# First norm of a decoder step on one Trainium2 core: raw rows transposed on arrival, the norm applied after the transposes, the kept rows added as the residual

## The reference

```python
def rmsnorm(x, g):
    xf = x.astype(jnp.float32)
    y = xf * lax.rsqrt(jnp.mean(xf * xf, axis=-1, keepdims=True) + EPS)
    return (y * g.astype(jnp.float32)).astype(x.dtype)

mp = mixer(rmsnorm(hp, norm_mix), ...)      # u @ w_in -> q, k, v, g, p, ga, gb; retention, pooling; @ w_out
hp = hp + mp                                # the residual
hp = hp + moe(rmsnorm(hp, norm_ffn), ...)   # top 4 of 32 experts, clamped SwiGLU
y  = rmsnorm(hp, norm_final)
```

## Time and profile before

| what | value |
|---|---|
| median of 3 runs | 1323.03 us (1321.56 to 1323.11) |
| the profiled execution, its own time | 1323.81 us |
| its span, first to last instruction | 1321.8 us |
| TensorE busy (matmul) | 1251.9 us, 95% |
| VectorE, ScalarE, GpSimd busy | 250.9, 168.0, 46.0 us |
| moved by DMA | 451.25 MB, mean 341 GB/s |

### The profile page before, as it was taken

One profiled execution on the slowest core, in us unless ns is written; L12 is line 12 of the kernel. 1 busy time (PEld: TensorE's weight loads), 2 busy tenths in 40 slices (PEclk: granted clock), 3 DMA queues, 4 the chain that ended last, 5 costly groups with the idle time before them and its releaser, 6 DMA issues.

```text
span 1321.8 us, 15582 instructions
## 1 busy us (share of the span) xinstructions
PE 1251.9 (95%) x5956; PEld 649.0 (49%) x5956; DVE 250.9 (19%) x579; ACT 168.0 (13%) x326; POOL 46.0 (3%) x81
## 2 busy tenths in 40 slices
PE   4999999998999999999999999999999999999984
PEld 3878678886434344443434344443434343443432
DVE  0143311203021211112121211212021211112022
ACT  3122211003101101110100110110100101001102
POOL 3014310000000000000000000000000000000000
PEclk9999999997899999999999999999999999999987
DMA  9552775431699999999999999999999999999980
GB/s 294 191 192 96 242 253 207 159 114 66 253 363 421 414 422 414 420 416 418 419 415 421 414 421 415 421 415 419 417 417 419 414 422 414 422 415 420 416 330 34
DMA packets 108060, 451.25 MB, mean 341 GB/s; under 512 B 7321, under 2 KB 38085, under 8 KB 75128
## 3 DMA queue, kind: packets, MB, share of 16 engines
q1 hardware_dynamic: 104704, 439.56, 83.0%
q0 software_dynamic: 3328, 11.30, 2.6%
HBM read 444.99 MB, written 6.08 MB: 341 GB/s over the span
## 4 chain that ended last, share of the span: by engine, by line
PE 77%; DMA 18%; DVE 2%; ACT 1%; issue 1%; SPq 0%; DVEq 0%; ACTq 0%
PE psum L780 23%; DMA ring<-in_w_down 18%; PE psum L727 18%; PE psum L796 15%; PE psum L819 11%; PE psum L845 5%; PE psum L809 1%; PE psum L834 1%; DMA tok<-in_meta_tokens 1%; PE psum L683 1%; PE psum L731 0%; PE psum L651 0%; PE psum L781 0%; PE psum L668 0%; PE psum L915 0%
## 5 line engine op out<-in xcount | busy, mean ns | idle before, releaser
L780 PE MATMUL psum<-ring,x_T 128*64 128x512 f32 x1024 | 462.3, 599 | 0.7 <-ACT x_T L1014 0.7
L781 PE MATMUL psum<-ring,x_T 128*64 128x512 f32 x1024 | 462.3, 599 | 0.0
L780 PEld LDWEIGHTS psum<-ring,x_T 128*64 128x64 f32 x1024 | 134.1, 137 | 273.3 <-issue 272.2
L796 PE MATMUL psum<-ring,act_T 128*64 128x512 f32 x1024 | 236.1, 603 | 25.3 <-DMA ring<-in_w_down 22.0
L727 PE MATMUL psum<-u_T,ring 128*128 128x264 f32 (+1 forms) x704 | 169.3, 395 | 0.0
L819 PE MATMUL psum<-one_hot,normed 128*128 128x128 f32 (+1 forms) x816 | 152.2, 317 | 1.2 <-DVE one_hot L1273 1.2
L796 PEld LDWEIGHTS psum<-ring,act_T 128*64 128x64 f32 x1024 | 73.3, 138 | 151.5 <-issue 145.8
L727 PEld LDWEIGHTS psum<-u_T,ring 128*128 128x128 f32 x704 | 131.6, 191 | 28.9 <-issue 3.5
L819 PEld LDWEIGHTS psum<-one_hot,normed 128*128 128x128 f32 (+1 forms) x816 | 115.5, 195 | 56.2 <-issue 27.7
L781 PEld LDWEIGHTS psum<-ring,x_T 128*64 128x64 f32 x1024 | 134.2, 137 | 0.0
L1343 DVE TENSOR_TENSOR z_T<-z_T,psum 128x264 f32<-128x264 f32 x136 | 58.3, 429 | 207.2 <-PE psum L845 206.1
(11 more groups left out here) (215 smaller groups left out, 544.1 us busy)
## 6 DMA issues: line engine op xcount, KB each, us to landing
ring<-in_w_gate_up SPq DMA_DIRECT2D x256, 1024.0 KB, 19.5
ring<-in_w_down SPq DMA_DIRECT2D x128, 1024.0 KB, 19.4
ring<-in_w_in SPq DMA_DIRECT2D x22, 1024.0 KB, 5.2
ring<-in_state_ret POOLq DMA_DIRECT2D x8, 512.0 KB, 6.2
out<-ring POOLq DMA_DIRECT2D x8, 512.0 KB, 4.3
ring<-in_w_ret_branch SPq DMA_DIRECT2D x4, 1024.0 KB, 5.0
ring<-in_w_out SPq DMA_DIRECT2D x4, 1024.0 KB, 5.0
ring<-in_w_pool_branch SPq DMA_DIRECT2D x2, 1024.0 KB, 8.0
```

The costliest lines, as they stand in the source:

```text
L780: mm(psum[0:CAP, 2 * j + n], x, slot(s)[:, n * 512:(n + 1) * 512], start=k == 0, stop=k == KD - 1)
L781: last = mm(psum[CAP:P, 2 * j + n], x, slot(s)[:, D + n * 512:D + (n + 1) * 512], start=k == 0, stop=k == KD - 1)
L796: last = mm(psum[j * CAP:(j + 1) * CAP, 4 + n], act_T[:, j, 2 * q + f], w[:, f * D + n * 512:f * D + (n + 1) * 512], start=q == 0 and f == ...
```

## The change

- The raw rows are transposed, tile by tile as each lands, all eight blocks into eight PSUM banks. ScalarE copies each block unscaled into a new buffer `x_kept` (1024 x 280, transposed). `tok` now lies in the space of `vk`, and is not needed after the head.
- The squares run beside this, three tiles, then one root instruction for all. VectorE's reciprocals are turned by three matmuls (reciprocals broadcast, times the identity) into a row that stands on all partitions, copied to `rstd_row`. VectorE then writes `u_T` = `x_kept` x `norm_mix` x `rstd_row`.
- The identity and eps come first in `consts` and are loaded alone by ScalarE's queue, the rest by SyncE's behind the second weight chunk. The four parameter rows move from GpSimd's queue to ScalarE's. x is loaded as two DMAs with their own semaphores. SyncE no longer waits for the parameter rows. An early root on ScalarE's stream brings its table in.
- The expert-bias transposes become an auxiliary job behind tile 4.
- In tiles 64 to 71 the identity matmuls go. VectorE adds `x_kept` while it takes the tile out into `y_T`; ScalarE scales that into `xn_T`. The waits for the bank and the logits follow.

```diff
+_aux(4, ("b_gu",), (7,))
-for _n, _w in (("ident", 128), ("before", 128), ...
-               ("of_row", NS), ("eps", 1)):
+for _n, _w in (("ident", 128), ("eps", 4), ("before", 128), ...
+               ("of_row", NS)):
+EARLY = CONST["before"][0]
-        tok = msb("tok", 3 * D).rearrange("p (t d) -> p t d", t=3)
+        x_kept = msb("x_kept", KD * NA).rearrange("p (k t) -> p k t", k=KD)
+        tok = vk[:, 0:3 * D].rearrange("p (t d) -> p t d", t=3)
+        rstd_row = win_all[:, 0:NA]
 ...
-            elif n < T_OUT:
+            else:
                 eng.wait_ge(dve_took, n - T_YB + 1)
-            else:
-                eng.wait_ge(act_took, T_YB + n - T_OUT + 1)
 SyncE
-            sp.dma_start(tok[:, 0:2, :], x_prompt[0].rearrange("(t p) d -> p t d", p=P)).then_inc(x_in, 16)
-            sp.dma_start(consts[:, :], ins["consts"]).then_inc(consts_in, 16)
-            sp.wait_ge(cleared, 1)
-            sp.dma_start(tok[0:NS, 2, :], x_sample.rearrange("b s d -> (b s) d")).then_inc(x_in, 16)
-            sp.dma_start(tok[32:32 + NM, 2, :], meta).then_inc(x_in, 16)
+            for t in range(2):
+                sp.dma_start(tok[:, t, :], x_prompt[0, t * P:(t + 1) * P, :]).then_inc(x_in[t], 16)
+            sp.wait_ge(cleared, 2)
+            sp.dma_start(tok[0:NS, 2, :], x_sample.rearrange("b s d -> (b s) d")).then_inc(x_in[2], 16)
+            sp.dma_start(tok[NS:NS + NM, 2, :], meta).then_inc(x_in[2], 16)
-            sp.wait_ge(rows_in, 4 * 16)
             for i in range(C_PB):
                 mix_chunk(i)
+                if i == 1:
+                    sp.dma_start(consts[:, EARLY:], ins["consts"][:, EARLY:]).then_inc(consts_in, 16)
 GpSimd
-            nc.gpsimd.memset(tok[0:64, 2, :], 0.0).then_inc(cleared, 1)
+            nc.gpsimd.memset(small[:, 0:4], 1.0).then_inc(cleared, 1)
+            nc.gpsimd.memset(tok[:, 2, :], 0.0).then_inc(cleared, 1)
-            for o, name, n in ((0, "norm_mix", 8), (8, "ret_gn", 8), (16, "pool_scale", 4), (20, "norm_ffn", 8)):
-                pool.dma_start(rows[o:o + n, 0:P], ins[name].rearrange("l (a p) -> (l a) p", p=P)).then_inc(rows_in, 16)
 TensorE, aux
+                elif kind == "b_gu":
+                    pe.wait_ge(b_gu_in, 16)
+                    for c in range(4):
+                        last = pe.transpose(banks(bank)[:, c * P:(c + 1) * P], rows[:, (1 + c) * P:(2 + c) * P], ident)
 TensorE, head (the loop quoted above and the b_gate_up transposes go)
-            pe.wait_ge(consts_in, 16)
+            pe.wait_ge(ident_in, 16)
             pe.wait_ge(rows_in, 4 * 16)
+            pe.transpose(psum[:, 7, 384:412], rows[0:28, 0:P], ident[0:28, 0:28]).then_inc(params_turned, 1)
+            for t in range(3):
+                pe.wait_ge(x_in[t], 32 if t == 2 else 16)
+                for k in range(KD):
+                    if t == 0 and k == KD - 1:
+                        pe.wait_ge(params_ready, 1)
+                    last = pe.transpose(psum[:, k, t * P:(t + 1) * P], tok[:, t, k * P:(k + 1) * P], ident)
+                    if t == 2:
+                        last.then_inc(x_turned, 1)
+            pe.wait_ge(rstd_ready, 1)
+            pe.wait_ge(kept, 1)
+            for t, n in enumerate((P, P, NS + NM)):
+                last = mm(psum[:, 0, t * P:t * P + n], rstd[:, t:t + 1].broadcast_to([P, P]), ident[:, 0:n], start=True,
+                          stop=True)
+            last.then_inc(rstd_turned, 1)
 TensorE, tiles
+                if n == 0:
+                    pe.wait_ge(rstd_row_ready, 1)
+                if n == 1:
+                    pe.wait_ge(kept, KD)
                 for k in range(nk):
+                    if n == 0:
+                        pe.wait_ge(u_ready, k + 1)
                     last = mm(o[:, 0:width], w[:, k, cols:cols + P], x[:, k, 0:width], start=k == 0, stop=k == nk - 1)
-                    if n >= T_OUT and k == 0:
-                        for t, (c0, m) in enumerate(TILES):
-                            mm(o[:, c0:c0 + m], tok[0:m, t, d * P:(d + 1) * P], ident[0:m, 0:m], start=False,
-                               stop=False)
-            pe.wait_ge(dve_took, T_END - T_YB)
+            pe.wait_ge(act_took, T_YB + T_END - T_OUT)
 ScalarE, head
+            act_e.dma_start(consts[:, 0:EARLY], ins["consts"][:, 0:EARLY]).then_inc(ident_in, 16)
+            for o, name, n in ((0, "norm_mix", 8), (8, "ret_gn", 8), (16, "pool_scale", 4), (20, "norm_ffn", 8)):
+                act_e.dma_start(rows[o:o + n, 0:P], ins[name].rearrange("l (a p) -> (l a) p", p=P)).then_inc(rows_in, 16)
+            act_e.wait_ge(cleared, 1)
+            step(A(small[:, 1:2], small[:, 0:1], ACT.Sqrt))
+            for t in range(3):
+                act_e.wait_ge(x_in[t], 32 if t == 2 else 16)
+                A(squares, tok[:, t], ACT.Square, accum_out=sumsq[:, t:t + 1]).then_inc(sq_done, 1)
+                act_e.wait_ge(sq_done, t + 1)
+            act_e.wait_ge(ident_in, 16)
+            A(rms, sumsq[:, 0:3], ACT.Sqrt, bias=const("eps")[:, 0:1], scale=1.0 / D).then_inc(rms_done, 1)
             for k in range(KD):
                 act_e.wait_ge(x_turned, k + 1)
-                A(u_T[:, k, 0:NT], psum[:, 4 + k % 4, 0:NT], ACT.Copy, scale=norm_mix[:, k:k + 1]).then_inc(u_ready, 1)
-                A(u_T[:, k, NT:NA], psum[:, 4 + k % 4, 288:304], ACT.Copy, scale=norm_mix[:, k:k + 1]).then_inc(
-                    u_ready, 1)
+                nc.scalar.copy(x_kept[:, k], psum[:, k, 0:NA]).then_inc(kept, 1)
 ScalarE, last eight tiles
-                act_e.wait_ge(tile_done, n + 1)
-                nc.scalar.copy(y_T[:, n - T_OUT], psum[:, n % 3, 0:NT]).then_inc(act_took, 1)
+                act_e.wait_ge(dve_took, n - T_YB + 1)
+                A(xn_T[:, n - T_OUT], y_T[:, n - T_OUT], ACT.Copy, scale=norm_ffn[:, n - T_OUT:n - T_OUT + 1]).then_inc(
+                    act_took, 1)
 VectorE, head
+            dve.wait_ge(rms_done, 1)
+            V.reciprocal(rstd, rms).then_inc(rstd_ready, 1)
+            dve.wait_ge(rstd_turned, 1)
+            V.tensor_copy(rstd_row, psum[:, 0, 0:NA]).then_inc(rstd_row_ready, 1)
+            dve.wait_ge(rstd_row_ready, 1)
+            for k in range(KD):
+                dve.wait_ge(kept, k + 1)
+                V.scalar_tensor_tensor(u_T[:, k], x_kept[:, k], norm_mix[:, k:k + 1], rstd_row, ALU.mult,
+                                       ALU.mult).then_inc(u_ready, 1)
 VectorE, last eight tiles
-                V.tensor_scalar(xn_T[:, n - T_OUT], y_T[:, n - T_OUT], norm_ffn[:, n - T_OUT:n - T_OUT + 1], None,
-                                ALU.mult).then_inc(dve_took, 1)
+                dve.wait_ge(tile_done, n + 1)
+                V.tensor_tensor(y_T[:, n - T_OUT], psum[:, n % 3, 0:NT], x_kept[:, n - T_OUT, 0:NT], ALU.add).then_inc(
+                    dve_took, 1)
```

More of the change, by code:

```diff
@@ L143 @@
 _o = 0
-for _n, _w in (("ident", 128), ("before", 128), ("ones", 128), ("twin", CAP), ("iota", CAP), ("experts", NE), ("passes", 8),
+for _n, _w in (("ident", 128), ("eps", 4), ("before", 128), ("ones", 128), ("twin", CAP), ("iota", CAP), ("experts", NE), ("passes", 8),
                ("cos", NA), ("sin", NA), ("mask", H * P), ("q_dec", H * P), ("k_dec", H), ("meta_dec", 1),
-               ("of_row", NS), ("eps", 1)):
+               ("of_row", NS)):
     CONST[_n] = (_o, _w)
@@ L328, in h_tok @@
             return banks((4, 6)[t], 2)
-        consts_in, x_in, rows_in, hist_in, misc_in, final_in = (
-            sem(n) for n in ("consts_in", "x_in", "rows_in", "hist_in", "misc_in", "final_in"))
+        x_in = [sem(f"x_in{t}") for t in range(3)]
+        ident_in, consts_in, rows_in, hist_in, misc_in, final_in = (
+            sem(n) for n in ("ident_in", "consts_in", "rows_in", "hist_in", "misc_in", "final_in"))
         wmix_in = [sem(f"wmix_in{s}") for s in range(MIX_SLOTS)]
@@ L337, in build @@
         stored, y_out = sem("stored"), sem("y_out")
-        cleared, x_scaled, sq_done, rms_done = (
-            sem(n) for n in ("cleared", "x_scaled", "sq_done", "rms_done"))
-        params_turned, params_ready, x_turned, u_ready = (
-            sem(n) for n in ("params_turned", "params_ready", "x_turned", "u_ready"))
+        cleared, sq_done, rms_done, rstd_ready, rstd_turned, rstd_row_ready = (
+            sem(n) for n in ("cleared", "sq_done", "rms_done", "rstd_ready", "rstd_turned", "rstd_row_ready"))
+        params_turned, params_ready, x_turned, u_ready, kept = (
+            sem(n) for n in ("params_turned", "params_ready", "x_turned", "u_ready", "kept"))
         tile_done, act_took, dve_took = sem("tile_done"), sem("act_took"), sem("dve_took")
@@ L1100, in aux @@
                     last = V.tensor_copy(k_few[32 * j:32 * j + NS + NM], ps[0:NS + NM, 2 * P:3 * P])
+                elif kind == "b_gu":
+                    last = V.tensor_copy(params[:, 28:28 + 512], ps)
                 elif kind == "hist":
@@ L1156, in group_norm @@
                 return last
-            dve.wait_ge(rms_done, 3)
```

(13 more changed lines are left out.)

47 lines of the change are left out of this document (12 added, 35 removed).

## The result

The changed kernel took 1304.04 us (median of 4 runs, 1303.09 to 1305.02) against 1322.3 for the kernel before beside it: a ratio of 0.9865, 95% interval 0.9848 to 0.9882. Run again with the experiments it took 1305.83 (1302.6 to 1308.02), ratio 0.987 [0.9853, 0.9886], a gain of 16.5 us.

What follows compares the result with a forecast made beforehand. It took TensorE's chain of waits, with an expert stage hung on its first matmul, as the bound. -8.57 + 1.2 + 0.45 - 6.08 + 0.05 = -12.95 from 1323.81 gave 1310.9, median 1310.1; range 1306 to 1315.5.

Steps and rivals of the forecast that it cites:

- The bound and the one-for-one shift: Whole kernel: the expert stage keeps its length and moves one for one with the first expert matmul.
- The last eight tiles, -6.03: Mixer's end: removing L731 saves 8 x 0.76 = 6.08 us, VectorE's adds hidden except +0.05 at the last.
- The start of the first tile, 17.5: Head: the first weight chunk lands at 17.5 us and sets the first projection tile, replacing 26.07, -8.57.
- TensorE's side, 15.9: Head: rows, raw transposes, row of roots and VectorE's first product ready at 15.9 us, ends 14.3 and 18.3.
- The slow beginning, +1.2: First projection tiles: TensorE idles beforehand and starts at its lower clock, losing 2.0 us, +1.2 against before.
- b_gate_up's transposes, +0.45: Behind tile 4: the four moved expert-bias transposes cost 4 x 0.11 us, +0.45.
- The last tile's exit, +0.05: End of the mixer: VectorE's add at 0.43 us instead of ScalarE's copy at 0.38, bare only at the last tile.
- (a): Head: GpSimd's traffic holds the first chunk until 20.6 us, +3.1, total 1313.2; chance 0.14.
- (c): Head: early issue buys little, chunk lands near 23.4 us as before, total 1315.9; chance 0.06.
- (b): Head: chunk slips in before GpSimd's traffic, TensorE's side sets the start at 14.3 us, total 1306.9; chance 0.14.
- (d): First tiles: clock stays low long after the idling head, 1318.6; chance 0.04 short of being slower than before, 0.02 past.
- the main case: Whole kernel: start 15.9 to 19, clock loss 0.8 to 2.9 us, total 1308 to 1312.5; chance 0.60.

Runs made afterwards that it cites:

- fill at the head: Changed kernel plus three unused 280-column matmuls between the head's last matmul and the first projection tile; 1304.97 us.
- held version: Changed kernel with GpSimd's loads from b_gate_up on held until the first weight chunk has landed; 1303.22 us.
- reordered version: Held version, but x's transposes don't wait for parameter rows, consts go behind the fourth chunk, GpSimd's loads wait for the third; 1301.28 us.
- best2: Reordered version plus unused wide matmuls in the routing before, between and after the groups of placement sums; 1292.71 us, ratio 0.9778.
- held_route: Held version plus unused wide matmuls in the routing, only before and after the placement sums; 1301.8 us, ratio 0.9836.

## Why the prediction was wrong, point by point

- *The bound and the one-for-one shift.* Right. The stage behind the first expert matmul kept its length (983.6 to 986.1 in the kernel before alone), and every variant's time followed its first expert matmul. Its spread of up to 3.6 us over all profiles was not allowed for; 2.2 us of the miss in the pair of profiles lie within that spread.
- *The last eight tiles, -6.03.* The mechanism was right, the size was not: 7.57 measured, 7.6 with the matmuls alone taken out. The step that failed is "8 x 0.76 = 6.08": the length that the chain gives a line is not what the line costs. The tile's own 16 records take 3.76 beside L731 and 3.56 without (VectorE's adds follow at 261.95, 265.51, 269.07). It is the one term that every profile shows as too small, but 1.5 us alone would have put the forecast at 1308.6, still inside the range; the rest of the miss is the early start and the spread of the expert stage, and only partly located (see the last point).
- *The start of the first tile, 17.5.* Near the mark in three of four profiles with these loads (17.0 to 17.3); the first profile's 15.7 is 1.8 under it. In part that is luck, since two terms were off and partly cancelled. GpSimd's flow was put at 5.9, from a lag of 3 us behind b_gate_up's issue; it began at 7.8, 5 us behind the queue's first issue. So SyncE's queue had moved 2.20 MB, the bytes of x and of the chunk if it serves its loads in order, at 13.0 and 13.3 us in the two profiles, where 16.2 was forecast. But the chunk was told landed only 2.7 and 4.0 us after that, not 1.3 (and by the rate used for it that lag was 1.6 already: consts is through at 7.6, not at 8). While GpSimd's queue flowed, SyncE's moved 0.11 to 0.15 MB per 2 us, the low end of what was taken. The decider, chunk or TensorE's chain, was named right: holding the loads moved the start to 14.20.
- *TensorE's side, 15.9.* Ready at 14.15. The 24 transposes took 4.95, not 6.3, and the six records of the row 0.75, not 1.6. It was not the later of the two sides, so this cost nothing.
- *The slow beginning, +1.2.* Near in size: 0.97 in the first pair, and 9.50 against 8.93, 0.57, in the second; with the head of before the first two tiles took 8.37, 8.93 and 9.18 in three executions. The reason given was wrong in one half: "the transposes alone won't have raised it". In both executions of the changed kernel they did: their weight loads go from 230 to 139 ns before 12.3, and the clock fell again in the wait or just behind it. In others, fill at the head among them, the loads stay at 230 ns to the last transpose, and the six records of the row right behind are faster by their end. The Trainium skill (TensorE: Matmul & The Clock Gate, "What's actually happening") has half clock after idling and full clock after sustained work. The windows of the changed kernel agree in kind: 1.00, then 0.50 around an idle of 2.55 us, and 1.00 again after some 3 us of tiles. These runs don't say how much idle it takes: after 4.30 us the clock still read 1.00 when the tiles began, and after 1.18 us it held in six profiles and fell in one.
- *b_gate_up's transposes, +0.45:* 0.44. *The last tile's exit, +0.05:* 0.45 - 0.38 = 0.07. Both right.
- *Rivals.* (a) and (c) did not happen. (b), the chunk in before GpSimd's traffic, is what the held version makes of it: 14.2, worked out at 14.3, but the number is luck: the parameter rows landed near 7.4, not at 5.5, and the shorter transposes made up for it. (d) at the head is ruled out, with a slow stretch of 3 us in place of 21; but its price in the routing is real: 6.5 us of gathers (15.07 to 8.53) and, with the rest of the routing, 8.6 us of the median between the reordered version and `best2`.
- *Two sums.* By its own terms the main case reaches down to 1307.3 (start 1.6 earlier, loss 1.2 less), not 1308. And if nothing were lost to the clock either now or before, the term is 0 and the time 1308.9; 1308.1 counts the 0.81 of before as gained.
- *The range.* Its low end took 1306.9 from rival (b) and left out that a term could be sized too low at the tail, and the spread of the expert stage. Tail 1.5, start 1.8, stage 2.2 and slow beginning 0.2 make 5.7 of the 5.9 us between 1310.9 and the profiled 1305.0. In the medians the change gave 5.3 us more than forecast the first time and 3.6 the second; the tail's 1.5 is in both, and where the other 3.8 and 2.1 lie is open, since the executions between the profiled ones left no trace. Another 0.7 us of the distance to 1310.1 is the kernel before itself, whose median over four runs is 1322.3 and not 1323.03.

## What to carry to other kernels

Price a group of instructions by the pitch of a tile of the same width with and without it, where the trace has both (3.56 and 4.52 here, both in the trace of before), not by the length that the chain puts on its line. At a kernel's head, what counts is which bytes stand ahead of the one chunk that the first matmul needs: loads that are wanted later belong behind it. One wait put them there and moved the first tile to 14.2; the median then fell by 2.6 us, which is not clear of the spread. Where narrow or idle stretches lie ahead of dense work on TensorE, look at the granted clock in windows of a few us; filling them with unused wide matmuls gave 8.6 us here, and filling half of them nothing that could be measured. One profile of a kernel is one draw: the same code had its chunk at 15.7 and at 17.3, and two kernels with the same head ran their first tiles at different clocks.

## What was not expected of the hardware

- GpSimd's queue began to flow 5 us after its first issue while SyncE's was full of packets (2.8 to 7.8 and 4.85 to 9.7), and under 3 us after it with SyncE's empty (2.8 to 5.5); SyncE's chunk began 4.2 us after its issue into GpSimd's flow (7.66 to 11.9). In the kernel before the first small packets of GpSimd's came after about 4 us. Why is not settled.
- The same chunk, with the same loads around it, landed 13.2, 14.5, 14.7 and 14.8 us after issue in four executions.
- In `held_route` the granted clock fell near 298.9 us, behind 2 us of matmuls of 32 columns and one group of wide ones; in `best2`, with wide ones between the narrow groups and less idle ahead of the gathers, it stayed at 1.00. One profile of each.
- The clock fell after 1.18 us of idle in one kernel and had not fallen after 4.30 us in another.
